# Sixty-four dot products move from the routing stage into the first seven expert pairs, mixing shifts to pairs 7 to 54, and three tiles' final norms stand beside the last pairs

## What is computed

```python
def one(args):
    hb, eb, gb = args
    ub = jnp.take(u_tab, eb, axis=0)
    vb = jnp.take(v_tab, eb, axis=0)
    a = jax.nn.gelu(jnp.einsum('nd,nhkd->nhk', hb, ub), approximate=False)
    return jnp.einsum('nhk,nhkd->nd', gb * a, vb)
```

## Time and profile before

| what | us |
|---|---|
| time of the runs: lowest, median, highest | 3455.19, 3460.2, 3461.52 |
| the profiled execution's own time | 3459.53 |
| its span, first to last instruction | 3457.9 |
| a routing period with 64 dots (the second one) | 122.28 |
| a routing period with neither dots nor one-hot rows (the last one) | 45.08 |
| an expert pair with mixing, and one without | 33.65, 29.53 |
| from PE's last matmul on the path to the end | 41.20 |

### The profile page before, as it was taken

The page is one execution under the profiler, slowest core; times in us unless marked ns, Lnnn a source line. Parts: engine busy times, 40 slices in busy tenths (PEclk is TensorE's granted clock), DMA queues, the critical chain, the costliest instruction groups (busy, mean ns, idle before and its releaser), DMA issues.

```text
span 3457.9 us, 45275 instructions
## 1 busy us (share of the span) xinstructions
PE 3047.9 (88%) x16658; PEld 2337.0 (68%) x16658; DVE 2417.9 (70%) x4977; ACT 935.4 (27%) x1272; POOL 1461.4 (42%) x1188
## 2 busy tenths in 40 slices
PE   8899969243888837999999999999999999999996
PEld 1466634121555536888887888888888888999995
DVE  1233316998888886777776777776777777888888
ACT  0111112012888852222222212222222222222222
POOL 0000001765554526555545455554555554333335
PEclk9999989676999978999999999999999999999998
DMA  9611151974222238999999999998999998777765
GB/s 359 190 62 61 55 189 61 317 264 160 104 104 104 104 146 333 340 326 335 334 323 322 332 339 324 338 326 314 356 330 336 323 339 302 235 233 235 238 231 201
DMA packets 305763, 858.06 MB, mean 248 GB/s; under 512 B 25360, under 2 KB 108816, under 8 KB 303840
## 3 DMA queue, kind: packets, MB, share of 16 engines
q0 software_dynamic: 151344, 551.09, 44.5%
q1 hardware_dynamic: 154189, 305.27, 25.7%
q10 hardware_dynamic: 108, 0.22, 0.0%
HBM read 793.34 MB, written 63.15 MB: 248 GB/s over the span
## 4 chain that ended last, share of the span: by engine, by line
PE 58%; DVE 1%; DMA 1%; POOL 1%; issue 1%; ACT 0%; DVEq 0%; SPq 0%
PE y_ps L1771 25%; PE a_ps L1752 25%; PE picked_ps L1789 5%; PE uT_ps L1739 3%; DMA shared<-in_peer_u,ids 1%; POOL shared L1428 0%; POOL quad L1438 0%; DVE shared L1711 0%; DMA quad<-in_peer_v,idsT 0%; DVE shared L1591 0%; DVE shared L1699 0%; DVE quad L1617 0%; DVE quad L1699 0%; DVE quad L1711 0%; DVE v_lo L1582 0%
## 5 line engine op out<-in xcount | busy, mean ns | idle before, releaser
L1428 POOL DMA_INDIRECT shared<-in_peer_u,ids x384 | 446.0, 1162 | 639.5 <-DVE acts L1604 593.2
L1752 PE MATMUL a_ps<-h_hi,uT_lo 128*128 128x320 f32 x2048 | 644.1, 314 | 1.7 <-DVE h_lo L1687 1.7
L1752 PE MATMUL a_ps<-h_hi,uT_hi 128*128 128x320 f32 x2048 | 634.3, 310 | 0.0
L1752 PE MATMUL a_ps<-h_lo,uT_hi 128*128 128x320 f32 x2048 | 634.2, 310 | 0.0
L1591 DVE TENSOR_TENSOR shared<-shared,y_ps 128x512 f32<-128x512 f32 x640 | 436.4, 687 | 270.7 <-PE y_ps L1771 270.5
L1771 PE MATMUL y_ps<-v_hi,m_lo 128*128 128x512 f32 x1280 | 510.1, 398 | 14.1 <-DVE shared L1591 8.9
L1771 PE MATMUL y_ps<-v_lo,m_hi 128*128 128x512 f32 x1280 | 505.1, 395 | 0.0
L1771 PE MATMUL y_ps<-v_hi,m_hi 128*128 128x512 f32 x1280 | 502.3, 392 | 0.0
L1604 DVE CUSTOM_DVE_ANT_0 shared<-shared 128x1024 f32<-128x1024 f32 x384 | 464.8, 1220 | 20.4 <-DMA shared<-in_peer_u,ids 20.4
L1438 POOL DMA_INDIRECT quad<-in_peer_v,idsT x384 | 405.3, 1056 | 117.9 <-issue 117.9
L1752 PEld LDWEIGHTS a_ps<-h_hi,uT_lo 128*128 128x128 f32 x2048 | 385.9, 188 | 7.1 <-issue 2.1
(11 more groups left out here) (181 smaller groups left out, 4473.8 us busy)
## 6 DMA issues: line engine op xcount, KB each, us to landing
shared<-in_peer_u SPq DMA_DIRECT2D x128, 512.0 KB, 6.5
v_all<-in_peer_v SPq DMA_DIRECT2D x128, 512.0 KB, 6.4
gate_blocks<-dense SPq DMA_DIRECT2D x10, 4096.0 KB, 12.6
gates<-gate_blocks SPq DMA_DIRECT2D x64, 640.0 KB, 17.5
w_ada<-in_w_ada SPq DMA_DIRECT2D x12, 2048.0 KB, 10.9
x_in<-in_x_prompt SPq DMA_DIRECT2D x16, 512.0 KB, 4.5
shared<-in_w_in SPq DMA_DIRECT2D x8, 768.0 KB, 12.4
shared<-in_peer_wq SPq DMA_DIRECT2D x3, 2048.0 KB, 14.0
```

The source lines that it names most:

```text
L1428: pool.indirect_dma_start(out=rows[n % 4], out_offset=None, in_=u_table if n < DOTS else v_table, in_offset=bass.IndirectOffsetOnAxis(ap=i ...
L1752: last = nc.tensor.matmul(a_ps[n][:, 0:GROUP], lhs[s][:, k, :], rhs[:, k, tok], start=k == 0 and m == 0, stop=k == KD - 1 and m == 2)
```

## The change

In `routing`, `dots` gives portions in the first of the two periods alone, so 64 dots of tile 0 instead of 128, and POOL gathers 64 rows there instead of 128. The other 64 dots of tile 0 become the first rows of `experts`: pairs 0 to 6 take them, pairs 7 to 20, 21 to 34 and 35 to 48 take the 128 dots of tiles 1, 2 and 3, and pairs 49 to 62 the 128 sums of tile 3 (`SPANS`). That is 576 rows in 63 pairs, nine in most pairs and ten in nine of them, where it was 512 in 64. Mixing stands in pairs 7 to 22, 23 to 38 and 39 to 54. `acts` has two halves, so the dots of a tile can run while the one before is mixed. The sum of tile 3 is kept in `token_row`, which frees the `quads`. After pair 56 SP loads what the end needs; tiles 0, 1 and 2 are gated by POOL after its gathers of pairs 57, 58 and 59, `x1` is added at the end of pairs 58, 59 and 60, ACT squares there, and DVE scales at the end of pairs 60, 61 and 62. The end after pair 63 has six tiles left. ACT's and SP's lists are written out instead of looped, and the index transposes of tile 3, which nothing read, lose one ACT copy.

```diff
+DOTS_EARLY = 64
...
 
-            if done is None or done >= 2:
+            if done != 0:
                 return range(0)
-            return range((done * BATCHES + b) * 4, (done * BATCHES + b) * 4 + 4)
+            return range(b * DOTS_EARLY // BATCHES, (b + 1) * DOTS_EARLY // BATCHES)
...
-            for slot in range(SLOTS):
+            for slot in range(DOTS_EARLY):
                 fetch(slot)
...
-    SEGMENT = PAIRS // PICKED
-    PER_PAIR = P // SEGMENT
-    DOTS = (PICKED - 1) * P
+    SEGMENT = 16
+    SPANS = (0, 7, 21, 35, 49, 63)
+    DOTS = PICKED * P - DOTS_EARLY
     ROWS = DOTS + P
+    MIX = SPANS[1]
+    MIX_END = MIX + MIXED * SEGMENT
     MIXED_PAIRS = MIXED * SEGMENT
+
+    def rows_before(c):
+
+        s = max(n for n in range(len(SPANS)) if SPANS[n] <= c)
+        start = max(s * P - DOTS_EARLY, 0)
+        if c >= SPANS[-1]:
+            return ROWS
+        count = P if s else P - DOTS_EARLY
+        return start + count * (c - SPANS[s]) // (SPANS[s + 1] - SPANS[s])
+
...
-        sums, added = quads[1][0], quads[0][3]
-
-
-        x1 = [sums, token_row, u[0], u[1]]
+        sums, added = quads[1][0], token_row
+
+
+        x1 = [sums, quads[0][3], sums, quads[0][3], *rows, sums]
...
-            return quads[0][t]
+            return added if t == MIXED else quads[0][t]
...
-            def pair(c, parity, half, s, opens=None):
-                last = isinstance(c, int) and c == PAIRS - 1
-                if opens is not None and 1 <= opens < PICKED - 1:
-                    sp.wait_ge(S.used, opens * P)
-                    sp.dma_start(token_row, h2_rows[opens + 1, :, :]).then_inc(S.row_in, 16)
-                if not last:
+            def pair(c):
+                parity = c % 2
+                if c in SPANS[1:PICKED]:
+                    t = SPANS.index(c)
+                    sp.wait_ge(S.used, rows_before(c))
+                    sp.dma_start(token_row, h2_rows[t, :, :]).then_inc(S.row_in, 16)
...
+            def load_last():
+
+                sp.wait_ge(mixed[0], MIXED_PAIRS)
+                sp.wait_ge(mixed[1], MIXED_PAIRS)
+                sp.dma_start(gate2[0], mod_rows[0, GATE2, :].partition_broadcast(P)).then_inc(S.gate2_0, 16)
+                sp.dma_start(g_last, g_final.partition_broadcast(P)).then_inc(S.g_last, 16)
+                for b in range(STREAMS):
+                    sp.dma_start(gate2[1][b * STEP:(b + 1) * STEP, :],
+                                 mod_rows[1 + b, GATE2, :].partition_broadcast(STEP)).then_inc(S.gate2_1, 16)
+                load_x1(1)
+                sp.wait_ge(S.sums_out, 16 * MIXED)
+                for t in range(MIXED):
+                    sp.dma_start(total(t), sums_rows[t, :, :]).then_inc(sums_in[t], 16)
+                load_x1(0)
+
...
+            for c in range(PAIRS):
+                pair(c)
+                if c == LAST:
+                    load_last()
+                if LAST + 2 <= c < LAST + 4:
+                    n = c - LAST
+                    sp.wait_ge(S.sumsq, n - 1)
+                    load_x1(n)
+            for n in range(max(PAIRS - LAST, 2), 4):
+                sp.wait_ge(S.sumsq, n - 1)
                 load_x1(n)
...
-            def fetch_half(c, half, n):
-
-                if c and c < MIXED_PAIRS:
-                    pool.wait_ge(mixed[half], c)
-                for step, q in enumerate((1, 2, None, 3, None, None, 0, None)):
-                    if q is None:
+            def fetch_half(c, half, rows):
+
+                mixes = MIX <= c < MIX_END
...
+                for q, after in ((1, 0), (2, 1), (3, 2), (0, len(rows) - 3)):
...
+            for c in range(PAIRS - 1):
+                ahead = range(rows_before(c) + 4, rows_before(c + 1) + 4)
+                fetch_half(c, 1, ahead[:len(ahead) // 2])
+                fetch_half(c + 1, 0, ahead[len(ahead) // 2:])
+                if c == LAST + 1:
+                    pool.wait_ge(S.gate2_0, 16)
+                    pool.wait_ge(S.zero, 2)
+                if LAST < c <= LAST + MIXED:
+                    gated(c - LAST - 1)
+                if LAST + 2 < c <= LAST + 2 + MIXED:
+                    root(c - LAST - 3)
...
+            def square(n):
+
+                act.wait_ge(S.summed, n + 1)
+                nc.scalar.activation(x1[n], total(n), ACT.Square, accum_out=sumsq[:, n:n + 1]).then_inc(S.sumsq, 1)
...
+                if LAST + 1 < c <= LAST + 1 + MIXED:
+                    square(c - LAST - 2)
...
+                todo = list(range(rows_before(c), rows_before(c + 1)))
+                late = c in SPANS[1:]
+
+                def uses(count):
+
+                    for n in todo[:count]:
+                        use(n)
+                    del todo[:count]
                 uT(c * 2 + 1, 1)
-                if not opens:
-                    use(c, 0)
-                    use(c, 1)
...
-                use(c, 0 if opens else 3)
+                uses(1)
                 collect(c - 1, 4)
-                if opens:
-                    use(c, 1)
+                if late:
+                    uses(1)
                 collect(c - 1, 5)
                 if c + 1 < PAIRS:
                     uT(c * 2 + 2, 0)
-                if opens:
-                    use(c, 2)
-                    use(c, 3)
-                use(c, 4)
+                uses(2)
+                if late:
+                    uses(1)
                 weigh(c, 1, 0)
                 collect(c - 1, 6)
-                use(c, 5)
+                uses(len(todo) - 2)
+                if LAST + 2 < c <= LAST + 2 + MIXED:
+                    mean_of(c - LAST - 3)
                 collect(c - 1, 7)
                 split_v(c, 0)
-                use(c, 6)
+                uses(1)
                 weigh(c, 1, 1)
                 collect(c - 1, 8)
                 collect(c - 1, 9)
-                use(c, 7)
+                uses(1)
                 split_v(c, 1)
                 rest(c, 1)
                 if not closes:
                     spread_half(c + 1, 0)
+                if LAST + 1 < c <= LAST + 1 + MIXED:
+                    add_x1(c - LAST - 2)
+                if LAST + 3 < c <= LAST + 3 + MIXED:
+                    normed(c - LAST - 4)
+
+            def add_x1(n):
+                dve.wait_ge(S.weighted, n + 1)
+                dve.wait_ge(x1_loaded[n], 16)
+                nc.vector.tensor_tensor(total(n), total(n), x1[n], ALU.add).then_inc(S.summed, 1)
...
+            collect(last, 0)
+            collect(last, 1)
+            add_x1(MIXED)
+            collect(last, 2)
+            collect(last, 3)
+            mean_of(MIXED)
+            add_x1(PICKED)
+            collect(last, 4)
+            collect(last, 5)
```

316 lines of the change are left out of this document (160 added, 156 removed).

## The result

The kernel after takes 3411.4 us (median of four runs, 3407.1 to 3413.6) where the kernel before, run beside it, takes 3459.5 us (3455.2 to 3461.5): a ratio of 0.986, interval 0.984 to 0.988, some 48 us faster. The prediction said 3386 us, 25 us less; the median lies 1.4 us above the upper end of its range. The profiled execution of after took 3407.1 us with a span of 3405.5, which is 52.4 us less than the 3457.9 of before.

The account below looks back on a forecast made before the run. The prediction took DVE to bound routing and PE the expert pairs, with PE waiting in only a few places. Its terms summed to -73.4 us, from 3459.5 us to 3386 us, range 3362 to 3410.

Parts of the forecast that it names:

- routing: Second dot period of routing: without its 64 dots it falls from 122.28 to 45.08 us, -77.2 us.
- start of the experts: Pair 0: no gathers of `quads`, so the second product comes 11.1 us earlier, less 1.9 for the clock; -9.2 us.
- one more mixing pair: Expert stage: one pair of 29.53 us becomes a mixing pair of 33.65 us, +4.1 us.
- steady pairs: Expert pairs with 9.14 rows instead of 8: PE doesn't see the extra DVE work and gathers; 0, from 0 to +18 us.
- where the dots change tiles: Openings at pairs 7, 21, 35, 49: the ninth row delays `m_lo`, 4.5 us each; +11 us net, between -7 and +25.
- last pairs: After pairs 57 to 60: POOL's multiplications slow DVE, and ACT's square waits for the `x1` addition; +6.8 us, 0 to +15.
- pair 63: Pair 63 loses its rows and three multiplications, so PE waits less for `m_lo`; -2.5 us, 0 to -5.
- end, to DVE's last instruction: After the last pair's second product: six tiles instead of nine, 38.9 us instead of 45.2; -6.4 us, 0 to -12.
- from there to the span's end: From DVE's last instruction to the span's end: the prediction had no term for it, counted as 0.
- rival (c): Mixing pairs: queues give no more than 330 GB/s, pairs last 35.5 us, kernel slower at 3477 us; chance 0.03.
- rival (b): Rows late in more places: 8 us at each opening, 2 us in each ten-row pair; 3418 us, chance 0.15.
- rival (a): The openings, where dots change tiles, are absorbed and the last pairs cost nothing; 3361 us, chance 0.15.

Follow-up runs that it names:

- norms_at_end: The kernel after with the multiplications, additions, squares, means and scalings of tiles 0 to 2 put back behind the last pair; 3404.6 us, one run.
- all_three: The kernel after with 6 rows in pair 0, 7 in pairs 7, 21, 35, 49, ACT's square and POOL's multiplication each moved later; 3372.4 us, one run.
- five_edits: all_three with SP's norm loads spread over three pairs and DVE's last collects ahead of the additions; median 3372.7 us, ratio 0.975 to the kernel before.

## Why the prediction came out 21 us short

Its terms, against the span of the profiled execution (the median of the runs is another 4.3 us longer):

| step | predicted, us | measured, us |
|---|---|---|
| routing | -77.2 | -76.7 |
| start of the experts | -9.2 | -7.5 |
| one more mixing pair | +4.1 | +4.1 |
| steady pairs | 0 | +0.1 |
| where the dots change tiles | +11 | +21.7 |
| last pairs | +6.8 | +12.8 |
| pair 63 | -2.5 | -0.5 |
| end, to DVE's last instruction | -6.4 | -9.2 |
| from there to the span's end | 0 | +2.8 |
| sum | -73.4 | -52.4 |

The step that failed is the price of a wait: in the mixing pairs behind the openings and in the last pairs the prediction charged PE's idle time alone, and the runs showed slow products behind it, 9.3 us at the openings and 3.7 in the last pairs, 13.0 of the 21.0 us. The mechanism of both terms was right.

- **Routing and steady pairs: right.** The period is 44.50 us (45.08 forecast). Mixing pairs stay at 33.65 us, pair 9 at 351 GB/s, and the pairs behind seven-row openings had 395 and 398 in the same 33.65 us, so rival (c), 330 GB/s and no more, is refuted, and so is the 2 us for ten-row pairs in rival (b). The Trainium skill, "DMA: Bandwidth & Descriptors", section "Specifications", gives a core about 358 GB/s, which the prediction weighed; these pairs lie above that figure too.
- **The start: mechanism right, wait larger.** The second product of pair 0 stands at 1261.45, 33.1 us behind the first transposition; the sum had 31.9. PE stood idle 4.32 us instead of 2.7 before it, and the slow clock behind it cost 2.65 instead of 1.9 us (36.50 - 29.53 - 4.32).
- **Where the dots change tiles: the term that was mis-sized most.** The mechanism, the ninth row ahead of `m_lo`, is the right one (seven rows remove the stall, the untouched opening keeps it). The size of the wait was right too: 4.23, 4.08, 4.14 and 5.97 us, 4.6 in the mean, where the prediction took 4.5. What it left out is what comes behind a wait. It had the price in hand: after pair 17's wait of 3.22 us it read a clock of 0.96 and 1.9 us from the earlier trace rows, and charged that at the start, but charged the four openings their wait alone. They cost 6.8, 6.6, 6.7 and 7.6 us, so 9.3 us in all went to the clock, and pair 7 and small delays added 1.2. Filling pair 22's wait with products took the surcharge away. Rival (b) had about the size (8 us each) with another cause, rows later still, and its ten-row part did not come.
- **The last pairs: right chain, low prices.** The prediction gave 2.6 us each to what follows pairs 58 and 59, from an addition of 1.2 to 2.7 us and a square in the way. The addition took 3.67 us: its own 1.22 and POOL's whole 2.41. PE's wait was 3.35 us, and the slow clock added 1.85: of the 6.0 us that were missing 1.5 are longer waits and 3.7 the clock. The prediction's sentence on the Trainium skill, "SBUF — State Buffer", section "Who interferes with whom" (an operation of DVE with two inputs from SBUF and one of POOL that reads SBUF exclude each other for a whole instruction), priced this at about 5 us more. Here the trace agrees with the page, but that the 5 us come near the 6.0 is luck, since the waits grew by 1.5 us only. The row of 2.76 us that the term went by met a part of a multiplication: it began at 3397.52, and POOL's instruction beside it ended at 3399.20. The `rest` of pairs 57 to 59, charged 0.6 us three times, was not hit. Pairs 57 and 58 lost 1.2 us to late transfers.
- **Pair 63: a collision overlooked.** 2.5 us were to come from the multiplications leaving that pair, and PE's wait for `m_lo` did fall from 5.06 us to 2.65. But a new one of 1.64 us stood in the same pair, so 0.5 us was left. In the kernel after, by time, POOL multiplies tile 3 as soon as the last row is used, and pair 62's `rest` on DVE runs beside it:

```profile
3332.33 3.29 POOL L1493 TENSOR_TENSOR shared<-shared,quad 128x1024 f32<-128x1024 f32 x1 [6.89 <-DVE shared L1670]
3333.29 3.00 DVE L1626 TENSOR_TENSOR m_lo<-m_all,m_hi 128x640 fp32r<-128x640 f32 x1
```

  The `rest` took 3.00 us instead of 0.82. In norms_at_end, where no multiplication stands there, it took 0.82, and PE did not wait.
- **The end: right by luck.** From the second product to DVE's last end it is 36.0 us, not 38.9, because tile 3's mean came 6.4 us after the start of the product instead of 9.3 (and 45.2 - 38.9 is 6.3, not 6.4). But the span ends 5.9 us behind DVE, 3.1 before, which the sum left out, and the two nearly cancel. POOL's last long instruction is a drain, shown here with its length in ns (shortest, median, longest) and its start in us, before and, in the second fence, after:

```profile
L1270 POOLq DRAIN  x1: 2281/2281/2281, 3452.1 to 3452.1; - x1
```

```profile
L1286 POOLq DRAIN  x1: 7611/7611/7611, 3397.6 to 3397.6; - x1
```

  In the kernel before the last store landed last (3457.50); in the kernel after it landed at 3402.16, and the drain lasted to 3405.2. In all_three and five_edits it took 9.82 us. What makes it longer was not shown.
- **The lower half of the range** rested on rival (a), openings absorbed; no opening was.
- The median is 4.3 us above the profiled execution. The stalls' spread between executions (162 to 167 us for the same four pairs) is large enough for that, and so is that of the stage's start (1228.4 to 1235.6 us); which of them it was is not shown.

## What to carry to other kernels

A wait of a saturated engine is priced with what comes behind it: here the pairs before the last in which PE waited 2.45 us or more lost 1.6 to 3.1 us beyond the wait, most of it in slow products, and a row of before had already shown it. Work moved to where an engine "has idle time" is placed by what stands behind it in that engine's order: nine rows fitted DVE's time in every pair, and still one of them, ahead of the instruction that PE waits for, cost 27.7 us at the four openings, 18.4 of waiting and 9.3 behind it; with seven rows there and ten in more of the other pairs 1.7 to 2.2 us were left, in pairs 36, 40 and 54. Two short steps of different engines in a row (a locked addition, a square ahead of copies) are found by moving each alone: either move took most of the loss. And a forecast is compared step by step, since a right sum (the end here) can hide two errors.
